# Down products of the feed-forwards: token tile by token tile inside each weight piece, in place of inner tile by inner tile

## The chip, the cores and the metric

The program runs on 1 core of one Trainium2 chip. The metric is the device time of one execution in microseconds (us), taken as the median of several runs. The kernel before took 3503.63 us (median of 3 runs, 3502.25 to 3514.58). The times and rows below come from one execution that was profiled on the chip.

## What is computed

The reference puts two blocks of two layers each one behind the other, on 512 tokens of width 1024 (and in the second block on 256 more context tokens). Every layer ends in a gated feed-forward with an inner width of 2816. Cut to that part, in float32:

```python
def first_block(x, ...):
    for l in range(2):
        ...
        h = rms_norm(x, ffn_norm[l])
        gate, up = jnp.split(h @ w_gate_up[l], 2, axis=-1)
        x = x + ((jax.nn.silu(gate) * up) @ w_down[l])
    return x

def _swiglu(h, w_gate, w_up, w_down):
    return (jax.nn.silu(h @ w_gate) * (h @ w_up)) @ w_down

def second_block(x, c, ctx, ...):
    for i in range(2):
        ...
        x = _layernorm(ALPHA * x + gt2 * _swiglu(x * (1 + sc2) + sh2, ...), ...)
        if i == 0:
            ctx = _layernorm(ALPHA * ctx + gt2c * _swiglu(ctx * (1 + sc2c) + sh2c, ...), ...)
    return x
```

The change concerns the last product of each of these four feed-forwards, hidden (tokens x 2816) times w_down (2816 x 1024). The output of the program is the 512 x 1024 result.

## The kernel before

The five engines each run an instruction list of their own, written out by hand; they meet at semaphores. TensorE is named PE in the rows, VectorE DVE, ScalarE ACT, GpSimd POOL. All weights stream through SBUF in pieces of 128 x 2048 float32 (1 MB), into a ring of three buffers (`k.ring`). For every piece VectorE makes two operands of lower precision whose sum is the piece: a rounded high part (CAST, L577, in `split_dve`; there are two buffers for it, `k.hi`) and the rest (L620, in `split_lo_dve`). The other operand of every large product is split in the same way, and `product3` (L563 to L565) multiplies high by high, high by low and low by high, three matmuls into one PSUM bank. This text calls the three matmuls of one `product3` a product.

**A feed-forward.** First come 22 pieces of gate and up weights, one per inner tile of 128 (`FT` is 22). ScalarE takes the gate from PSUM (L1669, in the second block's first layer L3546), VectorE multiplies it by the up part (L1705, L3579). Then come 12 pieces of down weights: for each of the two output halves `c` of 512 columns, six parts of four inner tiles (the sixth holds two). Before an inner tile can be an operand of a down product, ScalarE rounds it into a high part (L1686, or L3554) and VectorE subtracts that to get the low part (`low(j)`, L1696, or L3573). This text calls such a pair a hidden tile; `j` counts them from 0 to 43 over both halves. Hidden tiles live in a ring: ten pairs in `ffn_pe`, which serves the two layers of the first block and the last layer of the second (512 tokens, 4 token tiles of 128, `nt` is 4), and eight pairs and one for `j` 0 in `ffn_all_pe`, the first layer of the second block (768 tokens, 6 token tiles, `NT2`). The pairs lie in `hidden_operands` and `xt_operands`.

**The order around the change.** TensorE's loop in `ffn_pe` (L1641 to L1650) goes through the parts; in each it takes the piece (`take_split`, which waits until the low part of the piece is there), then the four inner tiles, and for each inner tile all token tiles (`down`, which waits for `hs_ready`, that is for VectorE's `low(j)`, and adds the product into the bank of that token tile). Parts 4 and 5 of the second half are written out behind that loop, in another order. `ffn_all_pe` has the same loop (L3519 to L3536), in which parts 0 and 5 of the second half go token tile by token tile.

**What TensorE gives back.** A list `k.later` holds signals that are put on the first two matmuls of each later product, one per matmul (`signal_later`): `hs_used` for a hidden tile that all its token tiles have used (ScalarE waits for it before it writes that place of the ring), and from `piece_used()` first the ring buffer (`empty`, for the DMA queue) and then `piece_used`, for which VectorE waits before it overwrites the high part of that piece.

**VectorE's order in the down part** is the same before and after. For a part with inner tiles 4p to 4p+3 it runs `low(4p)`, `low(4p+1)`, then the CAST of the next piece, then `low(4p+2)`, then the rest (L620) of the next piece, then `low(4p+3)`. The CAST of piece n writes the buffer of piece n-2, so it waits for `piece_used` of piece n-2, the piece just before the one that TensorE works on then:

```python
        low(j)
        ...
        if f % 4 == 1 and n < FT + 11:
            piece = split_dve(k, e, n, with_lo=False)
        if (f % 4 == 2 or f == FT - 1) and n < FT + 11:
            split_lo_dve(k, e, n, piece)
```

In the second half, `finish` is called behind inner tiles 3 to 6 and takes the first half's result out of PSUM: one addition (L1598) in the first block, three instructions (L3409, L3411, L3413) in the last feed-forward. In `ffn_all_dve` all six of them stand behind inner tile 3, with the whole split of the next piece ahead of them, and nothing is split between inner tiles 0 and 3 of that half. In the first block VectorE also does a sum that belongs to the second block (L1772), of which a few steps lie in the down part.

Of the kernel before, what the change touches and what calls it, by code (L numbers as in the profile page):

```python
# [34 lines left out]
NT2 = (SEQ + CTX) // P  # L35
# [5 lines left out]
FT = F // P  # L41
# [486 lines left out]
def take_split(k, pe, slot, n):  # L528

    pe.wait_ge(k.S.lo_ready, n + QUARTERS if n else 1)  # L530
    return k.hi[n % 2], k.ring_lo[slot[0] % RING]
# [8 lines left out]
def piece_used(k, slot, split=True):  # L540

    k.later.append(k.S.empty[slot[0] % RING])
    if split:
        k.later.append(k.S.piece_used)
    slot[0] += 1
# [1059 lines left out]
def ffn_pe(k, e, slot, xT, hs, nt, between=None, late=None, turn=None):  # L1605


    pe, S = e.eng, k.S

    def down(w, c, f, t):  # L1610
        j, n = FT * c + f, c * nt + t
        pe.wait_ge(S.hs_ready, j + 1)
        if f == 0 and c == 1:
            pe.wait_ge(S.hid_taken, FT)
        if f == 0 and c == 0 and between and t == 2:
            pe.wait_ge(S.ada_tr_taken, 2)
        if f == 0 and c == 1 and between and t == 3:
            pe.wait_ge(S.ada_taken, 3)
        last = product3(k, pe, k.ps[:, 4 * (1 - c) + t, :], pair(hs[j % len(hs)], slice(t * P, (t + 1) * P)),
                        pair(w, slice(512 * (f % 4), 512 * (f % 4) + 512)), f == 0, f == FT - 1)  # L1620
        if f == FT - 1:
            last.then_inc(S.mm_done, 1)

    for f in range(FT):
        w = take_split(k, pe, slot, f)
        if f >= 2:
            pe.wait_ge(S.hid_taken, f - 1)
        for half in range(2):
            for kt in range(KT):
                if turn and f == 0 and half == 0:  # L1630
                    turn.need(kt, 0)
                if f == 0 and kt % 4 == 0:
                    quarter_ready(k, pe, 2 * half + kt // 4)
                c = 1024 * half + kt * P
                last = product3(k, pe, k.ps[:, 2 * (f % 2) + half, 0:nt * P], pair(w, slice(c, c + P)), pair(xT, kt),
                                kt == 0, kt == KT - 1)
        piece_used(k, slot)
        last.then_inc(S.gate_ps, 1)
        if between:
            between(f)  # L1640
    for c, part in [(c, part) for c in range(2) for part in range(6)][:-2]:  # L1641
        w = take_split(k, pe, slot, FT + 6 * c + part)
        if late:
            late(c, part)
        for f in range(4 * part, min(4 * part + 4, FT)):
            for t in range(nt):
                down(w, c, f, t)
            k.later.append(S.hs_used)
        piece_used(k, slot)
    first = take_split(k, pe, slot, FT + 10)  # L1650
    slot[0] += 1
    second = None
    for t, part in ((0, 4), (1, 4), (0, 5), (1, 5), (2, 4), (2, 5), (3, 4), (3, 5)):
        if part == 5 and not second:
            second = take_split(k, pe, slot, FT + 11)
        for f in range(4 * part, min(4 * part + 4, FT)):
            down(second if part == 5 else first, 1, f, t)
    slot[0] -= 1
    for _ in range(2):
        piece_used(k, slot)  # L1660
# [1815 lines left out]
def down_job(c, t):  # L3476

    n = c * NT2 + t
    return n, n % 8


def ffn_all_pe(k, e, slot, _):
    pe, S = e.eng, k.S
# [3 lines left out]
    for f in range(FT):  # L3487
        w = take_split(k, pe, slot, f)
        if f >= 2:
            pe.wait_ge(S.hid_taken, f - 1)  # L3490
        for half in range(2):
            for s, (at, m) in enumerate(ALL_SEGS):
                for kt in range(KT):
# [4 lines left out]
                    c = 1024 * half + kt * P  # L3498
# [5 lines left out]
    def down(w, c, part, i, t):  # L3504
        f = 4 * part + i
        j = FT * c + f
        n, bank = down_job(c, t)
        pe.wait_ge(S.hs_ready, j + 1)
        if f == 0 and c == 0:
            pe.wait_ge(S.hid_taken, FT - 1 if bank < 4 else FT)  # L3510
        if f == 0 and c == 1 and t >= 2:
            pe.wait_ge(S.mm_taken, t - 1)
        last = product3(k, pe, k.ps[:, bank, :],
                        pair(hs_whole(k, j), slice(t * P, (t + 1) * P)),
                        pair(w, slice(512 * i, 512 * i + 512)), f == 0, f == FT - 1)
        if f == FT - 1:
            last.then_inc(S.mm_done, 1)

    for c in range(2):  # L3519
        for part in range(6):  # L3520
            w = take_split(k, pe, slot, FT + 6 * c + part)
            m = min(4, FT - 4 * part)
            if c == 1 and part in (0, 5):
                for t in range(NT2):
                    for i in range(m):
                        down(w, c, part, i, t)
                k.later.extend([S.hs_used] * m)
            else:
                for i in range(m):
                    for t in range(NT2):  # L3530
                        down(w, c, part, i, t)
                    k.later.append(S.hs_used)
            piece_used(k, slot)
    pe.wait_ge(S.mm_taken, NT1 + 1)
    spin_pe(k, pe, k.c2[:, 0:512], 4, 10)

# [593 lines left out]
```

## Time and profile before

| what | value |
|---|---|
| median of 3 runs | 3503.63 us |
| the profiled execution's own time | 3506.05 us |
| its span, first to last instruction | 3504.3 us |
| TensorE busy (matmuls) | 3385.8 us, 97% of the span |
| VectorE busy | 2083.1 us, 59% |
| ScalarE busy | 886.6 us, 25% |
| mean granted clock of TensorE | 0.99 of full |

The busy time of an engine says how much of the span it had an instruction in work; matmuls overlap in the pipeline, so their own durations add up to more than the time between their starts. "Idle before" is time in which an engine had nothing in work, and the name behind it says what ended that time. The granted clock of 1.0 is 2.4 GHz, 0.5 is 1.2 GHz.

### The profile page before, as it was taken

The numbers are of one execution on the slowest core, as the hardware profiler recorded it, in microseconds if no ns is written. First come the engines' busy times: TensorE is split into PE (matmuls) and PEld (weight loads), VectorE is DVE, ScalarE is ACT, GpSimd is POOL, SyncE is SP. The second block draws the span as 40 slices with busy tenths as digits, with TensorE's granted clock in tenths as the row PEclk, the third lists the DMA queues.
The fourth block names the chain that finished last, engine by engine and source line by source line (L and its number), as shares of the span: only waits on it lengthen the run. The fifth ranks groups of instructions, "written<-read, shape, count | busy, mean of one in ns | idle before, by whom it ended". The sixth has DMA issues, their size and how long they took to land.

```text
span 3504.3 us, 57388 instructions
## 1 busy us (share of the span) xinstructions
PE 3385.8 (97%) x24456; PEld 2791.8 (80%) x24456; DVE 2083.1 (59%) x2910; ACT 886.6 (25%) x1751; POOL 287.9 (8%) x263
## 2 busy tenths in 40 slices
PE   8999999999999999999999999999999999899998
PEld 6777888877778888788888877888888686678886
DVE  4665777646557776666676666322245744764347
ACT  2243001222430012455455421000021214610021
POOL 0000000000000000013203300300000002402000
PEclk9999999999999999999999999999999999999999
DMA  4311444323114543210110031111111421022222
GB/s 176 113 37 49 192 190 180 139 102 102 37 49 190 192 180 127 106 38 4 45 49 4 27 150 61 63 70 61 61 71 63 132 91 37 1 88 99 99 98 86
DMA packets 51454, 320.46 MB, mean 91 GB/s; under 512 B 7132, under 2 KB 7644, under 8 KB 16648
## 3 DMA queue, kind: packets, MB, share of 16 engines
q1 hardware_dynamic: 30492, 220.50, 17.1%
q10 hardware_dynamic: 20716, 96.36, 7.7%
q8 instruction: 193, 3.16, 0.4%
q14 instruction: 53, 0.43, 0.0%
HBM read 299.94 MB, written 9.56 MB: 88 GB/s over the span
## 4 chain that ended last, share of the span: by engine, by line
PE 78%; DVE 7%; PEld 6%; DMA 3%; issue 2%; ACT 2%; PEldq 1%; POOL 0%; POOLq 0%; ACTq 0%; another core or an unknown queue 0%; DVEq 0%; SPq 0%
PE psum L563 20%; PE psum L564 20%; PE psum L565 20%; PE psum L2700 3%; PE psum L2693 3%; DMA pieces_in<-pieces 2%; PEld psum L563 2%; PEld psum L565 2%; PEld psum L564 2%; PE psum L1406 1%; PE psum L1390 1%; PE psum L1379 1%; PE psum L760 1%; PE psum L3735 1%; PEldq L504 1%
## 5 line engine op out<-in xcount | busy, mean ns | idle before, releaser
L563 PE MATMUL psum<-xt_operands,pieces_hi 128*128 128x512 f32 (+1 forms) x2544 | 938.0, 369 | 19.6 <-DVE xt_operands L820 8.9
L564 PE MATMUL psum<-xt_operands,pieces_hi 128*128 128x512 f32 (+1 forms) x2544 | 927.3, 365 | 0.0
L565 PE MATMUL psum<-xt_operands,pieces_lo 128*128 128x512 f32 (+1 forms) x2544 | 927.0, 364 | 0.0
L563 PEld LDWEIGHTS psum<-xt_operands,pieces_hi 128*128 128x128 f32 x2544 | 480.7, 189 | 106.6 <-issue 15.2
L563 PE MATMUL psum<-pieces_hi,xt_operands 128*128 128x512 f32 x1338 | 531.0, 397 | 14.8 <-DVE pieces_lo L610 10.3
L565 PEld LDWEIGHTS psum<-xt_operands,pieces_lo 128*128 128x128 f32 x2544 | 480.5, 189 | 77.1
L564 PEld LDWEIGHTS psum<-xt_operands,pieces_hi 128*128 128x128 f32 x2544 | 481.1, 189 | 73.7
L565 PE MATMUL psum<-pieces_hi,xt_operands 128*128 128x512 f32 x1338 | 523.2, 391 | 0.0
L564 PE MATMUL psum<-pieces_lo,xt_operands 128*128 128x512 f32 x1338 | 523.1, 391 | 0.0
L620 DVE TENSOR_TENSOR pieces_lo<-pieces_in,pieces_hi 128x2048 fp32r<-128x2048 f32 x190 | 443.5, 2334 | 5.3
L577 DVE CAST pieces_hi<-pieces_in 128x2048 fp32r<-128x2048 f32 x190 | 237.7, 1251 | 300.1 <-PE psum L563 150.6
L563 PEld LDWEIGHTS psum<-pieces_hi,xt_operands 128*128 128x128 f32 x1338 | 253.0, 189 | 73.8 <-DVE pieces_lo L610 11.3
L564 PEld LDWEIGHTS psum<-pieces_lo,xt_operands 128*128 128x128 f32 x1338 | 252.9, 189 | 53.7 <-issue 2.4
L565 PEld LDWEIGHTS psum<-pieces_hi,xt_operands 128*128 128x128 f32 x1338 | 252.6, 189 | 53.5
L1669 ACT ACTIVATE arena<-psum 128x512 f32<-128x512 f32 x66 | 39.5, 598 | 673.8 <-PE psum L565 673.8
L1705 DVE TENSOR_TENSOR arena<-psum,arena 128x512 f32<-128x512 f32 x66 | 45.6, 692 | 247.1 <-ACT arena L1669 247.1
L3579 DVE TENSOR_TENSOR arena<-psum,arena 128x768 f32<-128x768 f32 x22 | 21.1, 958 | 256.1 <-ACT arena L3546 256.1
L2476 DVE SCALAR_TENSOR_TENSOR x_mem<-x_mem,arena 128x772 f32<-128x772 f32 x96 | 98.2, 1023 | 66.7 <-ACT x_mem L2375 64.1
L1686 ACT ACTIVATE xt_operands<-arena 128x512 fp32r<-128x512 f32 x102 | 59.8, 625 | 184.4 <-PE psum L563 146.1
L3546 ACT ACTIVATE arena<-psum 128x768 f32<-128x768 f32 x22 | 17.9, 812 | 341.9 <-PE psum L565 341.9
L1772 DVE SCALAR_TENSOR_TENSOR arena<-x_mem,xt_values,arena 128x2048 f32<-128x2048 f32 x44 | 101.9, 2346 | 2.3 <-DMA x_mem<-ada 2.3
L1772 DVE SCALAR_TENSOR_TENSOR arena<-arena,xt_values 128x2048 f32<-128x2048 f32 x40 | 92.1, 2345 | 0.0
(401 smaller groups left out, 4166.4 us busy)
## 6 DMA issues: line engine op xcount, KB each, us to landing
pieces_in<-pieces SPq DMA_DIRECT2D x210, 1024.0 KB, 4.8
x_mem<-ada ACTq DMA_DIRECT2D x28, 1024.0 KB, 4.8
arena<-ada ACTq DMA_DIRECT2D x20, 1024.0 KB, 4.8
arena<-mods ACTq DMA_DIRECT2D x8, 512.0 KB, 16.8
arena<-arena ACTq DMA_DIRECT2D x32, 128.0 KB, 4.9
xt_values<-arena ACTq DMA_DIRECT2D x8, 384.0 KB, 9.2
x_park<-x_mem ACTq DMA_DIRECT2D x1, 3072.0 KB, 14.1
o_park<-arena ACTq DMA_DIRECT2D x2, 1536.0 KB, 7.2
```

The source lines that it names most:

```text
L563: signal_later(k, pe.matmul(out, sh, mh, start=start, stop=False))
L564: signal_later(k, pe.matmul(out, sh, ml, start=False, stop=False))
L565: return pe.matmul(out, sl, mh, start=False, stop=stop)
L577: e.link(dve.tensor_copy(k.hi[n % 2], k.ring[i]))
L620: e.eng.tensor_tensor(k.ring_lo[i], k.ring[i], k.hi[n % 2].bitcast(F32), ALU.subtract).then_inc(k.S.lo_ready, 1)
L1669: act.activation(silu[:, f % 2, 0:nt * P], k.ps[:, 2 * (f % 2), 0:nt * P], ACT.Silu).then_inc(S.silu_ready, 1)
L1686: act.activation(hs[j % len(hs)][0], hid[:, j % FT, :], ACT.Copy).then_inc(S.hs_hi_ready, 1)
L1705: dve.tensor_tensor(hid[:, f, 0:nt * P], k.ps[:, 2 * (f % 2) + 1, 0:nt * P], silu[:, f % 2, 0:nt * P], ALU.mult).then_inc(S.hid_taken, 1)
L1772: eng.scalar_tensor_tensor(total, weights, c, total, ALU.mult, ALU.add).then_inc(added, 1)
L2476: ins = dve.scalar_tensor_tensor(conv, raw[:, j:j + 772], taps[:, n, j:j + 1], conv, ALU.mult, ALU.add)
L2693: last = pe.matmul(out, lhs(s, d, h), rhs(s, d, h), start=True, stop=True)
L2700: last = pe.matmul(out[r, h, :], lhs(h, r), rhs(h, r), start=True, stop=True)
```

## The change

In both functions the loops over inner tiles and token tiles change places, for all parts that go through these loops: TensorE now takes a token tile, does the four inner tiles of the piece in a row into that token tile's bank, and goes on to the next token tile. Since no hidden tile is done with before the last token tile, the four `hs_used` signals now stand together at the end of the piece, and behind the two signals of the piece in place of ahead of them. In `ffn_all_pe` the two parts that were written this way already keep their order; their signals change places too. Nothing else is edited: no instruction is added or removed, and VectorE's and ScalarE's lists are as before (their line numbers grow by one behind the edit in `ffn_pe`).

```diff
@@ ffn_pe
-        for f in range(4 * part, min(4 * part + 4, FT)):
-            for t in range(nt):
+        inner = range(4 * part, min(4 * part + 4, FT))
+        for t in range(nt):
+            for f in inner:
                 down(w, c, f, t)
-            k.later.append(S.hs_used)
         piece_used(k, slot)
+        k.later.extend([S.hs_used] * len(inner))
@@ ffn_all_pe
-            if c == 1 and part in (0, 5):
-                for t in range(NT2):
-                    for i in range(m):
-                        down(w, c, part, i, t)
-                k.later.extend([S.hs_used] * m)
-            else:
+            for t in range(NT2):
                 for i in range(m):
-                    for t in range(NT2):
-                        down(w, c, part, i, t)
-                    k.later.append(S.hs_used)
+                    down(w, c, part, i, t)
             piece_used(k, slot)
+            k.later.extend([S.hs_used] * m)
```

**A piece in the middle.** These are TensorE's rows at the start of part 2 of the first half, in the first feed-forward (inner tiles 8 to 11). Tiles 8 and 9 lie in `xt_operands`, tiles 10 and 11 in `hidden_operands`. Before:

```order
L563 MATMUL psum<-pieces_hi,xt_operands 128x512 [waits hs_ready,lo_ready]
L564 MATMUL psum<-pieces_lo,xt_operands 128x512
L565 MATMUL psum<-pieces_hi,xt_operands 128x512
L563 MATMUL psum<-pieces_hi,xt_operands 128x512 [waits hs_ready]
L564 MATMUL psum<-pieces_lo,xt_operands 128x512
L565 MATMUL psum<-pieces_hi,xt_operands 128x512
L563 MATMUL psum<-pieces_hi,xt_operands 128x512 [waits hs_ready]
L564 MATMUL psum<-pieces_lo,xt_operands 128x512
L565 MATMUL psum<-pieces_hi,xt_operands 128x512
L563 MATMUL psum<-pieces_hi,xt_operands 128x512 [waits hs_ready]
L564 MATMUL psum<-pieces_lo,xt_operands 128x512
L565 MATMUL psum<-pieces_hi,xt_operands 128x512
```

All four products are of tile 8, and four of tile 9 follow; tile 10 comes as the ninth product. The same rows after the change:

```order
L563 MATMUL psum<-pieces_hi,xt_operands 128x512 [waits hs_ready,lo_ready]
L564 MATMUL psum<-pieces_lo,xt_operands 128x512
L565 MATMUL psum<-pieces_hi,xt_operands 128x512
L563 MATMUL psum<-pieces_hi,xt_operands 128x512 [waits hs_ready]
L564 MATMUL psum<-pieces_lo,xt_operands 128x512
L565 MATMUL psum<-pieces_hi,xt_operands 128x512
L563 MATMUL psum<-pieces_hi,hidden_operands 128x512 [waits hs_ready]
L564 MATMUL psum<-pieces_lo,hidden_operands 128x512
L565 MATMUL psum<-pieces_hi,hidden_operands 128x512
L563 MATMUL psum<-pieces_hi,hidden_operands 128x512 [waits hs_ready]
L564 MATMUL psum<-pieces_lo,hidden_operands 128x512
L565 MATMUL psum<-pieces_hi,hidden_operands 128x512
```

Tile 10 has moved from the ninth product to the third, and tile 11 from the thirteenth to the fourth. VectorE's rows for the same inner tiles, after the change (tiles 7, 8 and 9 in the first row; L576 is the wait of `split_dve`):

```order
L1697 TENSOR_TENSOR xt_operands<-arena,xt_operands 128x512 [waits hs_hi_ready] x3
L576 ISA [waits slot_full2,piece_used]
L577 CAST pieces_hi<-pieces_in 128x2048
L1697 TENSOR_TENSOR hidden_operands<-arena,hidden_operands 128x512 [waits hs_hi_ready,dve_chain]
L620 TENSOR_TENSOR pieces_lo<-pieces_in,pieces_hi 128x2048
L1697 TENSOR_TENSOR hidden_operands<-arena,hidden_operands 128x512 [waits hs_hi_ready]
```

Nothing has moved here: tile 10 still stands behind the CAST that waits for `piece_used`, and tile 11 behind the L620 as well.

## Rows read from the trace of the kernel before

**Rows 1.** The page: busy us (share of the span) and instructions of each engine.

```profile
PE 3385.8 (97%) x24456; PEld 2791.8 (80%) x24456; DVE 2083.1 (59%) x2910; ACT 886.6 (25%) x1751; POOL 287.9 (8%) x263
```

**Rows 2.** The page: the chain that ended last, by engine.

```profile
PE 78%; DVE 7%; PEld 6%; DMA 3%; issue 2%; ACT 2%; PEldq 1%; POOL 0%; POOLq 0%; ACTq 0%; another core or an unknown queue 0%; DVEq 0%; SPq 0%
```

**Rows 3.** Waits of TensorE for hidden tiles, whole span: us in total, times, longest.

```profile
PE psum L563 <- DVE xt_operands L1696: 2.3, 2, 1.8
```

**Rows 4.** Timeline, TensorE, last feed-forward: starts of parts 0 and 2 (start, duration).

```profile
3368.54 0.39 PE L563 MATMUL psum<-pieces_hi,hidden_operands 128*128 128x512 f32 x1
...
3390.30 0.39 PE L563 MATMUL psum<-pieces_hi,xt_operands 128*128 128x512 f32 x1
```

**Rows 5.** Timeline, VectorE, same feed-forward, part 2 (idle before in brackets).

```profile
3391.51 1.23 DVE L577 CAST pieces_hi<-pieces_in 128x2048 fp32r<-128x2048 f32 x1 [4.92 <-PE psum L563]
3392.77 0.69 DVE L1696 TENSOR_TENSOR hidden_operands<-arena,hidden_operands 128x512 fp32r<-128x512 f32 x1
3393.38 2.28 DVE L620 TENSOR_TENSOR pieces_lo<-pieces_in,pieces_hi 128x2048 fp32r<-128x2048 f32 x1
3395.58 0.68 DVE L1696 TENSOR_TENSOR hidden_operands<-arena,hidden_operands 128x512 fp32r<-128x512 f32 x1
```

**Rows 6.** Timeline, ScalarE, same feed-forward: one rounding in part 2.

```profile
3390.79 0.63 ACT L1686 ACTIVATE xt_operands<-arena 128x512 fp32r<-128x512 f32 x1 [2.09 <-PE psum L563]
```

**Rows 7.** Timeline, VectorE, same feed-forward, part 0: hidden tiles 3 to 5.

```profile
3374.04 1.89 DVE L1696 TENSOR_TENSOR xt_operands<-arena,xt_operands 128x512 fp32r<-128x512 f32 x3
```

**Rows 8.** Timeline, VectorE, same feed-forward, second half, part 1.

```profile
3441.89 0.69 DVE L3409 TENSOR_TENSOR arena<-psum,arena 128x512 f32<-128x512 f32 x1
...
3443.95 0.68 DVE L1696 TENSOR_TENSOR xt_operands<-arena,xt_operands 128x512 fp32r<-128x512 f32 x1
...
3448.80 0.67 DVE L1696 TENSOR_TENSOR xt_operands<-arena,xt_operands 128x512 fp32r<-128x512 f32 x1
```

**Rows 9.** Timeline, TensorE, the same part: around its wait.

```profile
3447.35 0.39 PE L565 MATMUL psum<-pieces_hi,xt_operands 128*128 128x512 f32 x1
3449.53 0.50 PE L563 MATMUL psum<-pieces_hi,xt_operands 128*128 128x512 f32 x1 [1.79 <-DVE xt_operands L1696]
```

**Rows 10.** Timeline, VectorE, first feed-forward, second half, part 1.

```profile
670.00 0.69 DVE L1598 TENSOR_TENSOR x_mem<-psum,x_mem 128x512 f32<-128x512 f32 x1
670.61 0.68 DVE L1696 TENSOR_TENSOR xt_operands<-arena,xt_operands 128x512 fp32r<-128x512 f32 x1
```

**Rows 11.** Timeline, 768-token feed-forward: start (TensorE), tile 3 and part 1 (VectorE).

```profile
2541.85 0.40 PE L563 MATMUL psum<-pieces_hi,hidden_operands 128*128 128x512 f32 x1
...
2548.96 2.69 DVE L3573 TENSOR_TENSOR xt_operands<-arena,xt_operands 128x768 fp32r<-128x768 f32 x3
2559.51 1.23 DVE L577 CAST pieces_hi<-pieces_in 128x2048 fp32r<-128x2048 f32 x1 [7.86 <-PE psum L563]
...
2563.85 2.69 DVE L3573 TENSOR_TENSOR xt_operands<-arena,xt_operands 128x768 fp32r<-128x768 f32 x3
```

**Rows 12.** Windows, 768-token feed-forward, old and new order: length, PE busy (x), ..., PEclk, DMA.

```profile
2610.00:2620.00 10.00, 10.00 (x46) 8.29 (x45) 5.50 (x5) 1.71 (x3) 0.00 (x0) 1.00 0.22 92
2638.00:2648.00 10.00, 10.00 (x45) 8.26 (x44) 8.04 (x12) 0.00 (x0) 0.00 (x0) 1.00 0.00 0
```

**Rows 13.** Timeline, TensorE, elsewhere: long waits, and matmuls behind them.

```profile
109.32 0.50 PE L563 MATMUL psum<-pieces_hi,xt_operands 128*128 128x512 f32 x1 [2.86 <-DVE pieces_lo L610]
...
2100.92 0.62 PE L563 MATMUL psum<-pieces_hi,xt_operands 128*128 128x512 f32 x1 [0.93 <-DVE xt_operands L797]
...
2104.67 0.40 PE L563 MATMUL psum<-pieces_hi,xt_operands 128*128 128x512 f32 x1
3061.66 1.26 PE L760 MATMUL psum<-arena,xt_values 128*128 128x128 f32 x8 [1.43 <-DVE xt_values L3273]
```

**Rows 14.** Windows around these waits: the clock stands third from the end.

```profile
3064.00:3068.00 4.00, 2.13 (x9) 1.73 (x10) 4.00 (x9) 0.69 (x1) 0.00 (x0) 0.50 0.00 0
...
108.00:112.00 4.00, 2.68 (x12) 2.21 (x13) 4.00 (x9) 0.00 (x0) 0.00 (x0) 1.00 0.93 330
```

## The prediction

> **What bounds the kernel now.** I read the page first. TensorE has matmuls in work for 97% of the span [rows 1], and the chain of work that ended last runs through it for 78%, through VectorE for 7% [rows 2]. So whatever makes TensorE wait is paid in full, and work of VectorE is free as long as TensorE does not wait for it. Next I asked the waits what TensorE loses to hidden tiles today: 2.3 us in two waits over the whole program [rows 3]. The down parts run dense. From the start of part 0 to that of part 2 of the last feed-forward pass 21.76 us for 96 matmuls [rows 4], 0.227 us each, so 0.68 us a product and 10.9 us a piece of 16 products.
>
> Then the timeline of VectorE in one of these pieces [rows 5], which is the key to the change. Part 2 starts at 3390.30. VectorE sits idle for 4.92 us until TensorE gives back the piece before, and starts the CAST at 3391.51, 1.21 us into the part. Behind it stand the third hidden tile of this very part (3392.77), the L620 of the next piece, and the fourth hidden tile (3395.58, done 3396.26, 5.96 us into the part). In the old order the third tile is wanted after eight products, 5.44 us in, and the fourth after twelve, 8.16 us in, so both are in time. VectorE is fast enough, but by its order half of each part's tiles are made after the part has begun, and the old order hides that behind the four products that each tile feeds.
>
> **The change, step by step.** No instruction comes or goes; its steps are the wait at a piece, the places with more work in between, the signals, the bank and the clock.
>
> *An ordinary piece.* Now the third tile is wanted after two products, 1.36 us in, the fourth one product later. `piece_used` goes out earlier: it was third in the list behind the last `hs_used` and `empty`, so it rode on the fourth matmul; now it is second and rides on the second, two matmuls or 0.45 us sooner. So the CAST starts 1.21 - 0.45 = 0.76 us in. From the CAST's start to the end of the fourth tile pass 3396.26 - 3391.51 = 4.75 us [rows 5], and TensorE follows 0.06 us behind such an end (3448.80 + 0.67 against 3449.53 [rows 8, 9]). The fourth tile is there 0.76 + 4.75 + 0.06 = 5.57 us in; three products, 2.04 us, can be done before. TensorE loses 3.53 us, in two waits: 1.4 us for the third tile (0.76 + 1.26 + 0.69 + 0.06 = 2.77 us against 1.36) and 2.1 us for the fourth. A first matmul behind a wait has 0.50 us instead of 0.39 [rows 9], so I take 3.6 us a piece. The other 12 products run as before, and nothing gives the loss back, since the next CAST again waits for the end of this piece.
>
> The pattern holds for parts 1 to 4 of the first half and 0 to 3 of the second in each of three feed-forwards of 512 tokens. Part 5 has two tiles, both made ahead of the CAST, and the last two parts of the second half stay as they are. That is 24 pieces, of which three (part 1 of each second half) have `finish` steps in the chain: 21 x 3.6 = 75.6 us.
>
> *With `finish`.* Two of these steps stand between the CAST and the fourth tile. In the first block one is an addition of 0.61 us (670.00 to 670.61 [rows 10]): 3.6 + 1.2 = 4.8 us, twice 9.6. In the last feed-forward one is 2.06 us (3441.89 to 3443.95 [rows 8]): 3.6 + 4.1 = 7.7 us.
>
> *Part 0 of the first half.* Two tiles are made early, the others after the last gate. The fourth is done at 3374.04 + 0.68, so TensorE has it at 3374.78, 6.24 us after 3368.54 [rows 4, 7]; less 2.04, plus 0.1: 4.3 us, three times 12.9.
>
> *The 768-token feed-forward.* Eight pieces have the pattern (parts 1 to 4 of both halves). A tile takes VectorE 0.9 us, and from the CAST to the end of the fourth pass 2563.85 + 0.90 - 2559.51 = 5.24 us [rows 11]: 0.76 + 5.24 + 0.06 - 2.04 + 0.1 = 4.1 us, eight times 32.8. Its part 0 has one tile made early; the fourth is there at 2549.92, 8.07 us after 2541.85 [rows 11]: 6.1 us.
>
> *What goes.* The 2.3 us of waits of [rows 3] lie at two of these places and are replaced.
>
> *The later `hs_used`.* ScalarE waits for it 2.09 us before each rounding [rows 6], so it runs at the ring's limit, and that limit is six tiles ahead in the ring of ten. What is freed late now is wanted a piece or more later: nothing. If that cover were gone, a rounding of 0.63 us per tile would come on top. DMA pieces are given back as early as before: nothing.
>
> *One bank.* The bank is the only place for a gain. Part 0 of the second half in the 768-token feed-forward already has the new order: in 10 us TensorE has 45 matmuls in work there, in 10 us of the old order 46, both at full clock [rows 12]. I take nothing.
>
> The waits sum to 75.6 + 9.6 + 7.7 + 12.9 + 32.8 + 6.1 - 2.3 = 142.4 us.
>
> *The clock.* No row shows two waits of 1.4 and 2.1 us with one product between. From below: a single wait of 2.86 us in dense matmuls left the clock at full speed, 2.4 GHz [rows 13, 14]. From above: behind a wait of 1.43 us, 1.26 us of transposes and more waiting (2.13 us busy in the next 4), the clock stood at 0.50, that is 1.2 GHz [rows 13, 14]. A fall costs what a dense stretch at the low level shows: nine matmuls took 3.75 us (2100.92 to 2104.67 [rows 13]) instead of 2.04, so 1.7 us. The bounds are 0 and 36 places x 1.7 = 61 us. A piece's start looks more like the second row (two waits, little between), but its product is dense work, so I take 20 falls; part of the slow stretch lies inside the second wait, hence 1.5 us each: 30 us.
>
> In all 172 us. The profiled execution took 3506.05 us around its span of 3504.3; its sum is 3678. The median shown is 2.4 us lower, so the forecast for a median is **3676 us**, 4.9% slower.
>
> **The rivals.**
>
> A, the clock holds: 3503.6 + 142.4 = 3646 us. For it speaks the wait of 2.86 us that did nothing, against it the transposes' row.
>
> B, it falls at every piece: 3646 + 61 = 3707 us. For it speaks the transposes' row, against it the dense product between the waits. The Trainium skill ("TensorE: Matmul & The Clock Gate", section "A second HAM failure mode: psum-queue depth-cycling") tells of a kernel whose short idles between groups of matmuls sent the clock up and down and cost throughput; by that rule the time goes towards 3707 instead of 3646. No row here shows it for groups this size.
>
> C, not slower: VectorE's third and fourth tile are ready when a piece starts, because the CAST between is not held up. It decides if `piece_used` for the piece before came 4.2 us earlier (5.57 - 1.36): then TensorE never waits, and the old waits go too, 3503.6 - 2.3 = 3501 us. But the signal rides on a matmul behind that piece's last, and VectorE's idle 4.92 us show that it does wait for it [rows 5]. The Trainium skill's page "TensorE: Matmul & The Clock Gate" (section "Loop structure matters more than you think") gives as the good pattern what this change does: all inner tiles of an output tile in a row, the next output tile right behind. By that rule the time would stay at 3504 us or fall; the pattern supposes that the operands are there, and [rows 5] says that they are not.
>
> **How the numbers follow.** The forecast, waits in full and falls at part of the places: 0.58. A 0.22, B 0.15, C 0.03; 0.02 is left for a wait that I missed, beyond 3712. The terms of the sum are known to about 0.2 us a piece, some 7 us in all, so A reaches down to 3640 and B up to 3712: that is the range. About 0.5% is what a measurement of this kernel can tell from no change. Faster by that 0.01, the same 0.02 (C near 3501 is within it), slower 0.97.
>
> **What would show it.** In the waits of the new profile, TensorE should wait for L1697 (the low part, one line further) and L3568 or near (768 tokens) some 72 times, two per piece, near 1.4 and 2.1 us, together about 140 us. VectorE's idle time for `piece_used` per ordinary piece should grow from 4.92 to about 8.5 us, since its work stays and the piece gets longer. Pieces should start 14.5 us apart in place of 10.9. The windows over the down parts should show a granted clock under 1. I am wrong if TensorE waits for hidden tiles under 100 us in sum, if the pieces stay near 11 us, or if the time between matmuls within a bank is not 0.227 us.

## The result, and the profile of the kernel after

The kernel after takes 3721.86 us (median of 3 runs, 3719.07 to 3722.26) against 3503.63 before: 1.0606 times as long, 95% interval 1.0588 to 1.0623. The profiled execution took 3722.26 us. Direction and mechanism are as forecast; the size is 46 us above the 3676 and 10 us above the range.

The page of the kernel after: span, busy time by engine, the chain by engine, and the group that the first matmuls of the down products belong to (busy, mean ns, then idle before them).

```profile
span 3720.5 us, 57388 instructions
...
PE 3480.1 (94%) x24456; PEld 2839.4 (76%) x24456; DVE 2083.1 (56%) x2910; ACT 882.9 (24%) x1751; POOL 287.8 (8%) x263
...
PE 75%; DVE 11%; PEld 5%; DMA 3%; issue 3%; ACT 2%; PEldq 1%; POOL 0%; ACTq 0%; POOLq 0%; DVEq 0%; another core or an unknown queue 0%; SPq 0%
...
L563 PE MATMUL psum<-pieces_hi,xt_operands 128*128 128x512 f32 x1338 | 566.7, 424 | 126.9 <-DVE xt_operands L1697 82.2
```

The counts are those of [rows 1]. VectorE has the same 2083.1 us of work, but its share of the chain has gone from 7% [rows 2] to 11%. TensorE is busy for 94.3 us more (3480.1 - 3385.8) with the same 24456 matmuls: matmuls got longer. Waiting alone accounts for some 12 us of that (below, 73 waits at 0.16 us each). So there are two losses, and the next two views show one each.

Waits of the kernel after, TensorE's for hidden tiles and VectorE's for `piece_used` (total us, times, longest):

```profile
PE psum L563 <- DVE xt_operands L1697: 82.2, 48, 3.9
PE psum L563 <- DVE xt_operands L3568: 33.1, 19, 2.1
...
PE psum L563 <- DVE hidden_operands L1697: 9.2, 6, 1.8
...
DVE pieces_hi L577 <- PE psum L564: 362.8, 37, 16.3
```

Where 2.3 us stood [rows 3], there are 124.5 us in 73 waits. The rows count the time in which no matmul is in work, up to the next one's start; measured between the starts of matmuls each wait costs about 0.16 us more (below, 1.40 against 1.24), so some 136 us.

Timeline of VectorE, kernel after, the piece that [rows 5] show before (part 2 of the last feed-forward), and the next CAST:

```profile
3567.13 1.23 DVE L577 CAST pieces_hi<-pieces_in 128x2048 fp32r<-128x2048 f32 x1 [11.25 <-PE psum L564]
3568.39 0.69 DVE L1697 TENSOR_TENSOR hidden_operands<-arena,hidden_operands 128x512 fp32r<-128x512 f32 x1
3569.00 2.28 DVE L620 TENSOR_TENSOR pieces_lo<-pieces_in,pieces_hi 128x2048 fp32r<-128x2048 f32 x1
3571.20 0.68 DVE L1697 TENSOR_TENSOR hidden_operands<-arena,hidden_operands 128x512 fp32r<-128x512 f32 x1
...
3584.29 1.23 DVE L577 CAST pieces_hi<-pieces_in 128x2048 fp32r<-128x2048 f32 x1 [11.21 <-PE psum L564]
```

The same four instructions in the same 4.75 us as before. Only the idle time ahead of the CAST has grown, from 4.92 to 11.25 us, and the pieces are 17.16 us apart where they were 10.88. Timeline of TensorE in the same part, which starts at 3566.37 (start, duration, idle before):

```profile
3566.37 0.39 PE L563 MATMUL psum<-pieces_hi,xt_operands 128*128 128x512 f32 x1
...
3567.51 0.39 PE L565 MATMUL psum<-pieces_hi,xt_operands 128*128 128x512 f32 x1
3569.14 0.50 PE L563 MATMUL psum<-pieces_hi,hidden_operands 128*128 128x512 f32 x1 [1.24 <-DVE hidden_operands L1697]
...
3569.70 0.40 PE L565 MATMUL psum<-pieces_hi,hidden_operands 128*128 128x512 f32 x1
3571.94 0.80 PE L563 MATMUL psum<-pieces_hi,hidden_operands 128*128 128x512 f32 x1 [1.84 <-DVE hidden_operands L1697]
3572.53 0.63 PE L564 MATMUL psum<-pieces_lo,hidden_operands 128*128 128x512 f32 x1
...
3577.22 0.56 PE L563 MATMUL psum<-pieces_hi,hidden_operands 128*128 128x512 f32 x1
3577.62 0.40 PE L564 MATMUL psum<-pieces_lo,hidden_operands 128*128 128x512 f32 x1
3577.86 0.40 PE L565 MATMUL psum<-pieces_hi,hidden_operands 128*128 128x512 f32 x1
```

After two products TensorE's array stands for the third tile, does one product, and stands again for the fourth. From 3572.53 to 3577.22 the eleven steps between matmuls take 0.427 us each, at 1.2 GHz; then they are back near 0.227. Windows of the kernel after, one from CAST to CAST (length, busy time of each engine, granted clock third from the end), show this for piece after piece:

```profile
3549.92:3567.13 17.21, 14.13 (x50) 10.80 (x49) 5.93 (x7) 2.30 (x4) 0.00 (x0) 0.80 0.17 61
3567.13:3584.29 17.16, 14.08 (x50) 10.76 (x49) 5.92 (x6) 2.30 (x4) 0.00 (x0) 0.80 0.18 61
...
3623.95:3640.06 16.11, 13.03 (x50) 10.04 (x49) 9.87 (x12) 1.15 (x2) 0.00 (x0) 0.89 0.17 66
3640.06:3660.44 20.38, 13.21 (x50) 10.12 (x49) 9.87 (x12) 2.30 (x4) 0.00 (x0) 0.83 0.14 51
3660.44:3676.58 16.14, 13.06 (x50) 10.02 (x49) 5.92 (x6) 2.30 (x4) 0.00 (x0) 0.89 0.17 66
```

In windows of 0.4 us laid over the whole span, the kernel before has 10 stretches at half clock, 74 us in all, the kernel after 46 with 267 us. Of these 33 begin at one of the 36 places with late tiles: 23 last 6.7 us or more, 10 some 3.4 us; this text calls them long and short falls of the clock. Of the 36 places 29 are ordinary pieces (21 of 512 tokens, 8 of 768), 4 are starts of a first half and 3 have `finish` steps. The 29 hold 26 of the 33 falls: 18 of the 21, and all 8. The other 13 stretches of the kernel after have about the same time in sum as the 10 of before.

### The profile page after: what moved, and what is told of

Its sections match the earlier page's. It is cut to its first block, busy times and chain, and to the rows that moved or that the text cites. A ratio compares the mean times of both kernels' runs of the same rounds, so it can differ in the third digit from the quotient of the medians.

```text
span 3720.5 us, 57388 instructions
## 1 busy us (share of the span) xinstructions
PE 3480.1 (94%) x24456; PEld 2839.4 (76%) x24456; DVE 2083.1 (56%) x2910; ACT 882.9 (24%) x1751; POOL 287.8 (8%) x263
## 4 chain that ended last, share of the span: by engine, by line
PE 75%; DVE 11%; PEld 5%; DMA 3%; issue 3%; ACT 2%; PEldq 1%; POOL 0%; ACTq 0%; POOLq 0%; DVEq 0%; another core or an unknown queue 0%; SPq 0%
PE psum L563 20%; PE psum L564 19%; PE psum L565 19%; PE psum L2701 3%; PE psum L2694 2%; DVE pieces_lo L620 2%; DMA pieces_in<-pieces 2%; PEld psum L563 2%; PEld psum L565 2%; PEld psum L564 2%; PE psum L1406 1%; DVE pieces_hi L577 1%; PE psum L1390 1%; PE psum L760 1%; PE psum L1379 1%
## 5 line engine op out<-in xcount | busy, mean ns | idle before, releaser
L563 PE MATMUL psum<-pieces_hi,xt_operands 128*128 128x512 f32 x1338 | 566.7, 424 | 126.9 <-DVE xt_operands L1697 82.2
L564 PE MATMUL psum<-pieces_lo,xt_operands 128*128 128x512 f32 x1338 | 549.4, 411 | 0.0
L565 PE MATMUL psum<-pieces_hi,xt_operands 128*128 128x512 f32 x1338 | 547.9, 409 | 0.0
L620 DVE TENSOR_TENSOR pieces_lo<-pieces_in,pieces_hi 128x2048 fp32r<-128x2048 f32 x190 | 443.5, 2334 | 5.3
L563 PEld LDWEIGHTS psum<-pieces_hi,xt_operands 128*128 128x128 f32 x1338 | 269.9, 202 | 217.7 <-DVE xt_operands L1697 102.9
L565 PEld LDWEIGHTS psum<-pieces_hi,xt_operands 128*128 128x128 f32 x1338 | 268.1, 200 | 60.0
L564 PEld LDWEIGHTS psum<-pieces_lo,xt_operands 128*128 128x128 f32 x1338 | 269.8, 202 | 57.5 <-issue 2.4
```

Source lines behind the costliest of these rows:

```text
L563: signal_later(k, pe.matmul(out, sh, mh, start=start, stop=False))
L564: signal_later(k, pe.matmul(out, sh, ml, start=False, stop=False))
L565: return pe.matmul(out, sl, mh, start=False, stop=stop)
L620: e.eng.tensor_tensor(k.ring_lo[i], k.ring[i], k.hi[n % 2].bitcast(F32), ALU.subtract).then_inc(k.S.lo_ready, 1)
```

## The experiments

Two theories stood for the direction: the tiles come late because of VectorE's order (mine), or the new order costs something itself (so many products in a row in one bank, signals that come later). For the missing 46 us: the clock, or waits that I had not counted. The edits are shown against the kernel after unless said otherwise. Beside tiles_first, rest_last, only_768 and filler the kernel before took 3507.63 us, beside fill_third_only 3506.32, beside the other four 3507.98. The stretches at half clock are counted in each run's profiled execution, in windows of 0.4 us as above; the column behind them says how many begin at one of the 36 places, and in brackets how many of these are long.

| run | idle of TensorE in an ordinary piece | half-clock stretches, us | at the 36 places (long) | median us | ratio to before, interval |
|---|---|---|---|---|---|
| before | none | 10, 74 | 0 | 3503.63 | 1 |
| after | 1.24 + 1.84 | 46, 267 | 33 (23) | 3721.86 | 1.0606 [1.0588, 1.0623] |
| tiles_first | none at most pieces | 16, 109 | 1 (0) | 3517.70 | 1.0020 [1.0006, 1.0034] |
| vector_order_alone | none | 12, 86 | 0 | 3506.09 | 0.9994 [0.9983, 1.0004] |
| rest_last | 1.24 | 13, 86 | 2 (1) | 3580.76 | 1.0214 [1.0189, 1.0239] |
| two_token_tiles | 1.14 | 12, 72 | 1 (0) | 3585.23 | 1.0228 [1.0204, 1.0251] |
| only_768 | none (768 tokens as after) | 21, 135 | 9 (7) | 3566.10 | 1.0170 [1.0147, 1.0192] |
| filler | none, matmuls instead | 14, 81 | 5 (1) | 3656.73 | 1.0433 [1.0409, 1.0456] |
| fill_fourth_only | 1.24 | 19, 119 | 7 (1) | 3667.47 | 1.0440 [1.0414, 1.0466] |
| fill_third_only | 1.84 | 31, 168 | 19 (3) | 3688.97 | 1.0523 [1.0506, 1.0541] |
| one_wait | 3.44 | 41, 220 | 29 (10) | 3705.36 | 1.0561 [1.0539, 1.0584] |

### tiles_first: all four tiles ahead of the next piece's split

```diff
@@ ffn_dve (the same in ffn_all_dve)
-                if f % 4 == 1 and n < FT + 11:
-                    piece = split_dve(k, e, n, with_lo=False)
-                if (f % 4 == 2 or f == FT - 1) and n < FT + 11:
-                    split_lo_dve(k, e, n, piece)
+                if (f % 4 == 3 or f == FT - 1) and n < FT + 11:
+                    split_dve(k, e, n)
```

> The changed kernel, and VectorE splits the next weight piece (CAST and L620) behind the fourth hidden tile of a part instead of between its second, third and fourth. Theory (the loss comes from hidden tiles that are made after the part has begun; the clock falls because TensorE then idles): tiles of a part are ready when it starts, so the 3.5 us of waits at 32 pieces go, and the falls with them. Left are about 1.5 us at three starts, 2.6 at the start of the 768-token part, some 2 us at each of three parts that have other steps of VectorE ahead: 3515 us, between 3505 and 3530, granted clock 0.985 or above. Rival (four inner tiles in a row into one bank, or the late hs_used, cost by themselves): stays above 3650 us.

Measured: 3517.70 us, 1.0020. TensorE's list is that of the kernel after, word for word, and nearly all of the loss is gone. VectorE's timeline of this run in the last feed-forward:

```profile
3422.30 1.23 DVE L577 CAST pieces_hi<-pieces_in 128x2048 fp32r<-128x2048 f32 x1 [4.92 <-PE psum L564]
3423.56 2.29 DVE L620 TENSOR_TENSOR pieces_lo<-pieces_in,pieces_hi 128x2048 fp32r<-128x2048 f32 x1
3425.77 2.49 DVE L1697 TENSOR_TENSOR xt_operands<-arena,xt_operands 128x512 fp32r<-128x512 f32 x4
3433.18 1.23 DVE L577 CAST pieces_hi<-pieces_in 128x2048 fp32r<-128x2048 f32 x1 [4.92 <-PE psum L564]
```

The CAST still waits, 4.92 us as in [rows 5], but the four tiles behind it now belong to the next part, which has not begun. The pieces are 10.88 us apart. So the bank order and the later signals cost next to nothing, and nearly the whole effect of the change (204 of 218 us) goes through the tiles' lateness. What is left, some 7 to 10 us, has 7.7 us in 8 waits for tiles beside it, 2.06 us of them at the start of the 768-token layer.

### vector_order_alone: the same edit on the kernel before

The diff is the one above, put on the kernel before, TensorE in its old order.

> The kernel before, TensorE's order untouched, with VectorE's order of the run tiles_first: all four hidden tiles of a part first, the split of the next piece behind the fourth. Theory: in the old order no tile was late, so the earlier tiles have nothing to gain, and the next piece's split has still some 2 us to spare: 3507 us (3498 to 3518), not to be told from before. Rival: the few waits of before for hidden tiles (2.3 us) and more go away and it beats both kernels: under 3498 us; or the later split makes TensorE wait for the low part at the start of pieces: over 3520 us.

Measured: 3506.09 us, 0.9994, interval 0.9983 to 1.0004: no difference from before. With the tiles in time, the new order of TensorE is some 0.3% slower than the old one (3517.70 against 3506.09 us), and the 7.7 us of waits that tiles_first still has would be most of that. No run of the study is faster than the kernel before by more than its interval.

### rest_last and two_token_tiles: half of the lateness

```diff
@@ rest_last, ffn_dve (the same in ffn_all_dve)
-                if (f % 4 == 2 or f == FT - 1) and n < FT + 11:
+                if (f % 4 == 3 or f == FT - 1) and n < FT + 11:
                     split_lo_dve(k, e, n, piece)
@@ two_token_tiles, ffn_pe (the same in ffn_all_pe)
-        for t in range(nt):
+        for t in range(0, nt, 2):
             for f in inner:
-                down(w, c, f, t)
+                for u in (t, t + 1):
+                    down(w, c, f, u)
```

> The changed kernel, with L620 of the next piece moved behind the fourth hidden tile; the CAST stays ahead of the third. Theory (a wait for the third tile of about 1.4 us stays, the one for the fourth goes): 32 x 1.5 + 10 for the starts + 5 for the finish steps - 2 = 60 us of waits, and one short wait a piece leaves the clock up at most places: 3565 us, between 3550 and 3585. Rival (any wait at a piece's start brings the clock down): 60 + 33 x 2.4 = 140 us more, 3645 us.

> The kernel after, with TensorE taking two token tiles at a time: each hidden tile feeds two products before the next is wanted, so the third tile is wanted 2.72 us into a piece (there at 2.77), the fourth at 4.08 us (there at 5.57). Theory: only a wait of about 1.5 us a piece is left, 2 us in the 768-token layer, somewhat more at the starts and beside finish; in sum about 70 us, and few falls of the clock, as in the run rest_last: 3580 us (3565 to 3600). Rival: a wait of 1.5 us at each of 36 places brings the clock down as often as in the kernel after, 2 us each: 3650 us (3630 to 3670). If the time were set by how many products stand in a row in one bank, and not by when the tiles are there, it would lie half way, near 3615 us.

Measured: 3580.76 and 3585.23 us. Waits of TensorE in rest_last:

```profile
PE psum L563 <- DVE xt_operands L1697: 37.0, 28, 3.3
PE psum L563 <- DVE xt_operands L3568: 15.3, 10, 2.1
```

and in two_token_tiles:

```profile
PE psum L563 <- DVE xt_operands L1698: 35.1, 30, 3.2
PE psum L563 <- DVE xt_operands L3570: 15.1, 15, 1.4
```

With the smaller lines for `hidden_operands` (3.7 and 3.4 us) that is 56.0 and 53.6 us of idle time in 41 and 48 waits, or 63 and 61 us between starts. Two edits on different engines that leave waits of nearly the same length cost the same, 73 and 77 us, which is what a theory of lateness alone requires; both times lie in the range of that theory, and the rivals (3645, 3650 and 3615 us) do not hold. And both leave the clock almost as it was before (13 and 12 stretches): at the 29 ordinary pieces not one fall begins in either run. A window of rest_last over eight pieces of the 768-token layer, each with a wait of 1.51 us:

```profile
2580.00:2760.00 180.00, 167.92 (x724) 134.32 (x723) 79.51 (x73) 29.62 (x37) 0.00 (x0) 1.00 0.17 59
```
Some 13 and 18 us of these two differences are not accounted for by the waits (less the old 2.3 us); two_token_tiles ran from 3575.72 to 3595.46, and the profiled execution was its shortest.

### only_768: the new order in one layer

```diff
@@ ffn_pe: as in the kernel before
-        inner = range(4 * part, min(4 * part + 4, FT))
-        for t in range(nt):
-            for f in inner:
+        for f in range(4 * part, min(4 * part + 4, FT)):
+            for t in range(nt):
                 down(w, c, f, t)
+            k.later.append(S.hs_used)
         piece_used(k, slot)
-        k.later.extend([S.hs_used] * len(inner))
```

> Only the 768-token feed-forward has the new order; ffn_pe is as before the change. Theory (loss per place, waits of 4 to 6 us at nine places and a fall of the clock of some 2.5 us at each): 39 + 22 = 61 us more than before, 3565 us, between 3550 and 3575. Rival (the loss is one of the whole program, by the clock's state): above 3600 us or no different from before.

Measured: 3566.10 us, 58.5 above before. The loss is local: its waits for L3567 are 33.2 us in 19, as in the kernel after, and there are 21 stretches at half clock against 10, one at each of the nine places. Nine places cost 6.5 us each, waits and clock together.

### filler: the waits stay, the array works through them

```diff
@@ ffn_pe
+    def busy(w, j, bank, count):
+        if bank == 5:
+            pe.wait_ge(S.mm_taken, 2)
+        for _ in range(count):
+            pe.matmul(k.ps[:, bank, :], pair(hs[j % len(hs)], slice(0, P))[0], pair(w, slice(0, 512))[0], start=True, stop=True)
...
         for t in range(nt):
             for f in inner:
+                if t == 0 and f % 4 >= 2 and c + part:
+                    busy(w, FT * c + f - 1, (0, 2, 5)[0 if c == 0 else 1 if part == 0 else 2], (5, 8)[f % 4 - 2])
                 down(w, c, f, t)
```

and the like in `ffn_all_pe`. Five and eight unused matmuls stand in the two waits.

> The changed kernel with matmuls that nobody uses put into its waits: 5 ahead of the third hidden tile's first product and 8 ahead of the fourth's (0.227 us each, into a bank that is free), at 32 pieces; the four starts of the first halves stay bare. Theory (the clock falls because TensorE idles at the start of the piece): the tiles come as late as before, so the waits of about 142 us stay, now filled, but the clock holds at these pieces: 3503.6 + 142 + about 17 for the places left bare = 3660 us, between 3640 and 3680; pieces 14.5 us apart. Rival (the clock falls for another reason than idling, or the excess over 142 us is not the clock's): 3720 us or more, pieces 17.1 us apart.

Measured: 3656.73 us. Timeline of TensorE in this run (L1628 are the unused matmuls):

```profile
3513.70 1.29 PE L1628 MATMUL psum<-pieces_hi,xt_operands 128*128 128x512 f32 x5
3515.10 0.50 PE L563 MATMUL psum<-pieces_hi,hidden_operands 128*128 128x512 f32 x1
...
3515.92 2.02 PE L1628 MATMUL psum<-pieces_hi,hidden_operands 128*128 128x512 f32 x8
3517.91 0.50 PE L563 MATMUL psum<-pieces_hi,hidden_operands 128*128 128x512 f32 x1
```

and its window from CAST to CAST:

```profile
3513.09:3527.65 14.56, 14.45 (x63) 11.29 (x62) 5.93 (x6) 2.31 (x4) 0.00 (x0) 1.00 0.20 72
```

The tiles come as late as before, the useful work of a piece takes as long, and 13 matmuls per piece have been added; yet the program is 65 us faster than the kernel after. A piece takes 14.56 us instead of 17.16, at full clock. So the loss of the change has two parts: the waits, and the clock. The split at 149 us (filler less before) and 65 us gives the clock a little too small a share: five places in filler still have a fall, its four bare starts and one `finish` piece, where the unused matmuls leave waits of 2.15 and 2.06 us. At the prices of the next section these are some 9 us of the 149. In the pieces of the 768-token layer they leave 0.38 and some 0.25 us.

### fill_fourth_only, fill_third_only and one_wait: which idle time costs the clock

```diff
@@ fill_fourth_only, against filler
-                if t == 0 and f % 4 >= 2 and c + part:
+                if t == 0 and f % 4 == 3 and c + part:
@@ fill_third_only, against filler
-                if t == 0 and f % 4 >= 2 and c + part:
+                if t == 0 and f % 4 == 2 and c + part:
@@ one_wait, ffn_dve (the same in ffn_all_dve)
-                if f % 4 == 1 and n < FT + 11:
-                    piece = split_dve(k, e, n, with_lo=False)
-                if (f % 4 == 2 or f == FT - 1) and n < FT + 11:
-                    split_lo_dve(k, e, n, piece)
+                if (f % 4 == 1 or f == FT - 1) and n < FT + 11:
+                    split_dve(k, e, n)
```

> The kernel after, with unused matmuls only in the second wait of a piece (8 ahead of the fourth tile's first product at 32 of the 36 places), none in the first: the wait of 1.4 us for the third tile is left as idle time. The sum of the waits stays. If a single short wait is passed over by the clock: 3657 us (3645 to 3675), as the run filler. If the first wait alone is enough to bring the clock down at most places: 3715 us (3695 to 3730), as the kernel after.

> The counterpart of fill_fourth_only: unused matmuls only in the first wait of a piece (5 ahead of the third tile's first product at 32 of the 36 places), none in the second, so that 2.1 us of idle time for the fourth tile are left, with a product and the unused matmuls ahead of it. The sum of the waits stays. Theory: how often the clock falls grows with how long the array goes without work; idle times of 1.4 us cost next to nothing (fill_fourth_only, 1.044 of before), 3.6 us in one or two pieces cost about 55 to 65 us (one_wait, the kernel after); 2.1 us lie between, nearer the first: 3675 us (3655 to 3695). Rival: the last wait of a piece decides by itself: 3715 us (3700 to 3730). Other rival: only both together bring the clock down: 3660 us, no more than fill_fourth_only.

> The kernel after, with VectorE's L620 moved ahead of the third hidden tile, so that CAST and L620 both run ahead of the last two tiles of a part. The third tile should then come 0.76 + 1.26 + 2.2 + 0.69 + 0.06 = 5.0 us into a piece, 3.6 us after it is wanted, and the fourth right behind, so that TensorE has one wait of 3.6 us in place of two of 1.4 and 2.1 us with a product between. My theory (TensorE waits as long in sum, and loses the clock behind it): waits near the same sum, and if one long wait brings the clock down as two short ones do, 3720 us (3700 to 3735). Rival: it is the pair of waits that brings the clock down, a single one is passed over (as the row of 2.86 us in the trace of before was): 3655 us (3640 to 3675).

Measured: 3667.47, 3688.97 and 3705.36 us. All three lie in the range of the theory, and the rivals (a first wait that is enough, a last wait that decides, a single wait that is passed over) fall. By the medians, against filler, the wait of 1.24 us alone costs 11 us, that of 1.84 us alone 32, one of 3.44 us 49, and the two of the kernel after together 65. By the ratios, each to the runs of before beside it, they cost 2, 32, 45 and 61 us. So the first can't be told from nothing (the intervals of filler and fill_fourth_only overlap almost in full). The traces, place by place, agree. The two single waits, in fill_fourth_only and in fill_third_only:

```profile
3525.87 0.50 PE L563 MATMUL psum<-pieces_hi,hidden_operands 128*128 128x512 f32 x1 [1.24 <-DVE hidden_operands L1705]
...
647.09 0.50 PE L563 MATMUL psum<-pieces_hi,xt_operands 128*128 128x512 f32 x1 [1.84 <-DVE xt_operands L1705]
```

| run | wait in an ordinary piece of 512 tokens: falls | of 768 tokens: falls |
|---|---|---|
| fill_fourth_only | 1.24 us: 0 of 21 | 1.51 us: 0 of 8 |
| fill_third_only | 1.84 us: 12 of 21 | 2.10 us: 0 of 8 |
| one_wait | 3.44 us: 14 of 21 | 3.71 us: 8 of 8 |
| after | 1.24 and 1.84 us: 18 of 21 | 1.51 and 2.10 us: 8 of 8 |

The falls of fill_fourth_only lie at its starts and its `finish` pieces alone. On the whole falls get more frequent with longer waits, as my theory had it, but length is not all: the waits of 2.10 us in fill_third_only bring none, those of 1.84 us bring twelve. Windows of fill_third_only, over the eight pieces with 2.10 us, then over the first feed-forward:

```profile
2653.00:2845.00 192.00, 172.16 (x740) 137.38 (x739) 75.94 (x70) 29.61 (x37) 0.00 (x0) 1.00 0.15 55
604.00:700.00 96.00, 85.63 (x349) 65.04 (x348) 52.52 (x49) 15.70 (x28) 0.00 (x0) 0.95 0.34 123
```

What makes the difference is not shown by these runs. one_wait is 15 us below the value I gave: its stretches at half clock are nearly as many (41) but shorter in sum (220 us). Timeline of TensorE in one_wait:

```profile
3575.17 0.50 PE L563 MATMUL psum<-pieces_hi,xt_operands 128*128 128x512 f32 x1 [3.44 <-DVE xt_operands L1697]
...
3575.99 0.61 PE L563 MATMUL psum<-pieces_hi,xt_operands 128*128 128x512 f32 x1
...
3579.63 0.40 PE L563 MATMUL psum<-pieces_hi,xt_operands 128*128 128x512 f32 x1
```

and of VectorE around it:

```profile
3570.96 1.23 DVE L577 CAST pieces_hi<-pieces_in 128x2048 fp32r<-128x2048 f32 x1 [8.67 <-PE psum L564]
...
3587.20 1.23 DVE L577 CAST pieces_hi<-pieces_in 128x2048 fp32r<-128x2048 f32 x1 [10.27 <-PE psum L564]
...
3601.86 1.23 DVE L577 CAST pieces_hi<-pieces_in 128x2048 fp32r<-128x2048 f32 x1 [8.70 <-PE psum L564]
```

The first of these two pieces has a fall of about 3.4 us, all of it in working time, and takes 16.24 us; the second has none and takes 14.66. A short fall costs 1.6 us. A long one, as in the piece shown of the kernel after, costs 17.16 - 14.56 = 2.6 us. An estimate from these prices and the falls at the 36 places gives 3, 24, 47 and 67 us more than filler for the four runs of the last table, near what the times show.

## Why the prediction was wrong in size

**The waits: right.** In the piece shown the CAST starts 0.76 us into the part (3567.13 - 3566.37), as forecast. TensorE waits 1.40 us for the third tile (3569.14 - 3567.51 - 0.23) and 2.01 us for the fourth (3571.94 - 3569.70 - 0.23); 1.4 and 2.1 were forecast. At full clock pieces are 14.56 us apart in filler, and VectorE idles 8.56 to 8.60 us there: 14.5 and 8.5 forecast. (In the kernel after itself the piece shown takes 17.16 us and VectorE idles 11.25, with the clock's share on top.) 73 waits were seen where some 72 were forecast, with about 136 us where the sum, with the old 2.3 us back in, had 144.7: some 8 us less, which hid a part of the error below. The forecast named as a sign of error a time between matmuls within a bank that is not 0.227 us. It is 0.427 us at half clock and 0.227 again behind it, so that sign shows the clock here, and not the bank.

**Finish, part 0, 768 tokens: right.** The `finish` piece of the last feed-forward takes 20.38 us: 10.88 + 7.7 by the forecast, and 1.8 us of clock. The 768-token layer waits 33.1 us in 19, or 36 between starts; 38.9 were forecast, and half of the difference is its part 0, with some 4.6 us for 6.1.

**One bank, late `hs_used`: right, nothing.** tiles_first holds both, at 1.0020.

**The clock: the step that failed.** I took 20 falls at 1.5 us each, 30 us, with 36 x 1.7 = 61 us as the end of the range. The runs give 65 us (after less filler, which keeps some 9 us of falls itself), the rows 23 x 2.6 + 10 x 1.6 = 76 us, and the profiled execution, as what is left of its 216.2 us after 134 us of new waits, 82 us. Two things were off. The number: 33 places fell, not 20. The 20 was a choice between two rows, and the one that spoke for fewer, the wait of 2.86 us that left the clock alone [rows 13, 14], was one draw (last section). And the price: the stretch that I priced it from, nine matmuls in 3.75 us [rows 13], is a short one of some 3.4 us, and 23 of the 33 were long. The long kind stood in the trace of before: six of its ten stretches last some 6.8 us, two still longer (one of 13.7 us of small matmuls, one at the program's end), and the prediction used none of them as a price. Its timeline of TensorE elsewhere shows one of 6.8 us, behind a wait of 4.62 us:

```profile
1724.45 0.80 PE L563 MATMUL psum<-xt_operands,pieces_hi 128*128 128x512 f32 x1 [4.62 <-DVE pieces_lo L610]
1725.05 0.63 PE L564 MATMUL psum<-xt_operands,pieces_hi 128*128 128x512 f32 x1
...
1728.89 0.50 PE L564 MATMUL psum<-xt_operands,pieces_hi 128*128 128x512 f32 x1
```

with this window of before (clock third from the end):

```profile
1722.00:1728.80 6.80, 4.35 (x10) 3.47 (x11) 5.73 (x18) 0.21 (x1) 0.00 (x0) 0.52 0.88 365
```

From 1725.05 to 1728.89 nine steps take 0.427 us each, at half clock, behind a long stretch inside the wait. Half of a stretch of 6.8 us is 3.4 us, which would have been a safer price for the upper bound: 36 x 3.4 = 122 us and a range up to about 3770. So 61 us was no bound; it was one example multiplied.

**The rivals.** A, the clock holds, 3646 us: not what happened, but filler makes it happen and takes 3656.73. B, a fall at every piece, 3707 us: nearest of the cases, nearly right in the count (33 of 36), 15 us short by the same price. The rule of the Trainium skill named there ("TensorE: Matmul & The Clock Gate", section "A second HAM failure mode: psum-queue depth-cycling") agrees with this trace: short idles between groups, the clock down and up at 33 of 36 places, about 65 us. I gave it 0.15 and my mixed case 0.58. The row of the transposes, with little work between waits, came out nearer; that the little work is the reason is not shown, since one_wait has a single wait and falls at 29 places. C, not slower: its condition does not hold in the kernel after, but tiles_first fulfils it, and then the time is 3517.70. There the pattern of the same page ("Loop structure matters more than you think"), which the change follows inside a piece of four inner tiles, costs next to nothing, and gains nothing either.

## What to carry to other kernels

An order of loops has a demand side: before turning it, set down for each operand when it is wanted and when its maker can have it, with the wait that the maker itself stands behind. Here the wanted time of the fourth tile went from 8.16 to 2.04 us against 5.57 us, and moving TensorE's order alone lost 6%, moving both 0.2%. Where waits come at regular places in dense TensorE work, price the clock as well, from the longest low stretch that the trace shows in such work, and not from one row in which it held or one short fall. Then test the price: here a single wait of 1.24 us per piece brought no fall, two of 1.24 and 1.84 us one at nearly every piece.

## What was not expected of the hardware

**The same wait, with and without a fall.** The wait of 2.86 us for the low part of a piece [rows 13], where the clock stayed at 1.00 [rows 14], stands in a stretch of the program that the change does not touch. In the profiled execution of the kernel after, its timeline and its windows read:

```profile
108.41 0.50 PE L563 MATMUL psum<-pieces_hi,xt_operands 128*128 128x512 f32 x1 [2.86 <-DVE pieces_lo L610]
```

```profile
108.00:110.00 2.00, 1.59 (x6) 1.30 (x7) 2.00 (x5) 0.00 (x0) 0.00 (x0) 0.91 1.01 408
110.00:112.00 2.00, 2.00 (x6) 1.52 (x6) 1.97 (x3) 0.69 (x2) 0.00 (x0) 0.50 1.14 283
```

The same length to 0.01 us, and the clock fell to half. Of the eleven profiled executions of this study three show a fall there, eight none. The three are those in which the wait ends earliest (at 108.19, 108.41 and 108.76; the others at 109.11 to 109.99). What decides it is not settled by these runs; it was not tried to move that wait in time alone.

**Unused work made the program faster.** 32 times 13 unused matmuls in the waits took 65 us off the kernel after. This repairs only the clock, though: making the tiles in time takes off 204 us.

**Idle time and clock loss are not in proportion.** One wait of 1.24 us per piece brought no fall at any of 29 pieces, one of 1.84 us brought 12 at 21, and one of 2.10 us none at 8. A single wait of 3.44 us cost less clock than 1.24 and 1.84 us with three matmuls between (by the medians 49 against 65 us), though it is longer than their sum.
